# The output projection of each mixer layer in two turns by tokens, with the first turn's norm, residual and next inputs or stores beside the second

## The reference, cut to what matters

```
def merge_branches(...):
    m = (sigmoid(ga) * ((ya * silu(za)) @ w_branch[0]) + sigmoid(gb) * (...) + sigmoid(gc) * (...))
    return m @ w_o

def mixer_layer(x, ctx, ...):
    hx = rms_norm_2(x, g_pre) * (1.0 + scale_x) + shift_x
    hc = rms_norm_2(ctx, g_pre) * (1.0 + scale_c) + shift_c
    ... = in_proj(hx, w_in), in_proj(hc, w_in)
    ...
    out_x = merge_branches(...)
    x = x + gate_x * rms_norm_2(out_x, g_post)
    if update_ctx:
        ...
        ctx = ctx + gate_c * rms_norm_2(out_c, g_post)
    return x, ctx
```

## Time and profile before

| what | value |
|---|---|
| median of 3 runs | 2620.71 us (2618.78 to 2623.35) |
| the profiled execution | 2622.16 us, span 2620.4 us, mean granted TensorE clock 0.967 |
| PE busy | 2471.9 us, 94% of the span |
| DVE, ACT, POOL busy | 1179.1, 916.0, 531.7 us |
| chain that ended last | PE 85%, DVE 6%, ACT 4%, POOL 2%, issue 2%, DMA 1% |

### The profile page before, as it was taken

The page is one execution under the profiler, slowest core; times in us unless marked ns, Lnnn a source line. Parts: engine busy times, 40 slices in busy tenths (PEclk is TensorE's granted clock), DMA queues, the critical chain, the costliest instruction groups (busy, mean ns, idle before and its releaser), DMA issues.

```text
span 2620.4 us, 34188 instructions
## 1 busy us (share of the span) xinstructions
PE 2471.9 (94%) x14039; PEld 1979.8 (76%) x14039; DVE 1179.1 (45%) x1849; ACT 916.0 (35%) x1576; POOL 531.7 (20%) x381
## 2 busy tenths in 40 slices
PE   7887888899999999999999999999989999999998
PEld 5665666677788876678877888888866677878876
DVE  3745555353433445562267223323457633733432
ACT  3324543242222234552146211113335533632223
POOL 3003222040200212230014110022332210321023
PEclk8997899899999999999999999999989999999998
DMA  5231133145443321001300212123021023023232
GB/s 166 65 115 33 33 118 125 64 153 169 133 140 97 104 63 41 25 17 49 97 25 2 65 57 81 46 67 113 27 85 33 25 65 113 9 65 109 76 110 83
DMA packets 195740, 200.60 MB, mean 77 GB/s; under 512 B 15832, under 2 KB 189624, under 8 KB 195330
## 3 DMA queue, kind: packets, MB, share of 16 engines
q1 hardware_dynamic: 191106, 178.23, 21.7%
q10 hardware_dynamic: 4480, 20.19, 2.0%
HBM read 187.92 MB, written 10.49 MB: 76 GB/s over the span
## 4 chain that ended last, share of the span: by engine, by line
PE 85%; DVE 6%; ACT 4%; POOL 2%; issue 2%; DMA 1%; POOLq 0%; ACTq 0%; SPq 0%; DVEq 0%
PE PS L719 20%; PE PS L720 20%; PE PS L722 20%; PE PS L837 5%; PE PS L867 4%; PE PS L851 3%; DVE WL L1888 1%; PE PS L798 1%; PE PS L910 1%; ACT WH L1317 1%; PE PS L966 1%; PE PS L923 1%; PE PS L937 1%; POOL RB L2638 1%; PE PS L775 1%
## 5 line engine op out<-in xcount | busy, mean ns | idle before, releaser
L719 PE MATMUL PS<-HH,WH 128*128 128x512 f32 (+2 forms) x2096 | 776.0, 370 | 13.4 <-POOL HL L2791 6.6
L720 PE MATMUL PS<-HL,WH 128*128 128x512 f32 (+2 forms) x2096 | 744.9, 368 | 0.0
L722 PE MATMUL PS<-HH,WL 128*128 128x512 f32 (+2 forms) x2096 | 675.2, 366 | 0.0
L1888 DVE TENSOR_TENSOR WL<-WB,WH 128x2048 fp32r<-128x2048 f32 (+3 forms) x158 | 324.1, 2051 | 676.0 <-ACT WH L1317 666.5
L719 PEld LDWEIGHTS PS<-HH,WH 128*128 128x128 f32 (+1 forms) x2096 | 394.2, 188 | 124.3 <-issue 11.1
L720 PEld LDWEIGHTS PS<-HL,WH 128*128 128x128 f32 (+1 forms) x2096 | 394.2, 188 | 73.5 <-issue 2.9
L722 PEld LDWEIGHTS PS<-HH,WL 128*128 128x128 f32 (+1 forms) x2096 | 356.9, 188 | 45.1
L1317 ACT ACTIVATE WH<-WB 128x2048 fp32r<-128x2048 f32 (+3 forms) x158 | 265.1, 1678 | 343.4 <-PE PS L722 275.7
L2663 POOL TENSOR_SCALAR SA<-SA,ST 128x768 f32<-128x768 f32 (+4 forms) x80 | 142.2, 1778 | 533.2 <-DVE ST L1969 533.2
L2638 POOL TENSOR_TENSOR RB<-RB,SA 128x512 f32<-128x512 f32 (+2 forms) x65 | 88.2, 1357 | 399.2 <-ACT SA L1336 330.2
L1957 DVE TENSOR_REDUCE ST<-PS 128x1 f32<-128x768 f32 (+4 forms) x176 | 129.9, 738 | 71.4 <-PE PS L837 57.9
(11 more groups left out here) (366 smaller groups left out, 3641.1 us busy)
## 6 DMA issues: line engine op xcount, KB each, us to landing
WB<-in_w_in_dram SPq DMA_DIRECT2D x61, 1024.0 KB, 5.1
WB<-in_w_ff_dram SPq DMA_DIRECT2D x32, 1024.0 KB, 5.5
WB<-in_w_mod_dram SPq DMA_DIRECT2D x24, 1024.0 KB, 5.3
WB<-in_w_branch_dram SPq DMA_DIRECT2D x24, 512.0 KB, 3.5
WB<-in_w_o_dram SPq DMA_DIRECT2D x8, 1024.0 KB, 5.1
WB<-in_w_in_dram SPq DMA_DIRECT2D x14, 512.0 KB, 5.0
XTc<-xd ACTq DMA_DIRECT2D x2, 3072.0 KB, 10.0
WB<-in_cmp_w_dram SPq DMA_DIRECT2D x4, 1024.0 KB, 5.6
```

What stands on the lines that cost most here:

```text
L719: pe.matmul(D[0:m, d + o:d + o + w], h, xh[:, o:o + w], start=first, stop=False)
L720: pe.matmul(D[0:m, d + o:d + o + w], h, xl[:, o:o + w], start=False, stop=False)
L722: t = pe.matmul(D[0:m, d + o:d + o + w], lo, xh[:, o:o + w], start=False, stop=last)
L1888: dve.tensor_tensor(b.of(WL[s % NH]), b.of(WB[b.n % NW]), b.of(WH[s % NH]).bitcast(F32), ALU.subtract).then_inc(*done("wl", s))
```

## The change

The output projection of each layer is done in two turns. In layer 0 the first turn (`x`) does the 512 latent tokens and the second (`c`) the 256 context tokens; in layer 1 the turns are tokens 0 to 255 and 256 to 511. The first turn takes the output tiles 0 to 7, the second 4, 5, 6, 7, 0, 1, 2, 3: weight blocks 2 and 3 are used while they are still split, and blocks 0 and 1 are loaded and split once more, so each layer has 6 loads and splits of `w_o` in place of 4. Both turns use two of the four PSUM buffers. Beside the second turn run, tile by tile in each queue (`beside`), the first turn's sums, norm, residual and, in layer 0, the next inputs of `x` (`next_inputs`, `next_high`), in layer 1 its transposes, copies and stores. In layer 1 `linear_pair("ql1")` needs only the inputs of `x`; the context's sums follow it, the context's inputs are made beside the third tile of `ql1` and the first part of `kvl1`, which is now done by token sides (`linear_sides`). Buffers in SBUF are laid out anew for this.

```diff
-        cut(f"o{l}", I["w_o_2"][l])
+        for u in range(6):
+            i = u if u < 4 else u - 4
+            name = f"o{l}" if u < 4 else f"o{l}c"
...
+        TURNS = {0: {"x": (0, NX, 0), "c": (NX, NC, 1)}, 1: {"x": (0, 256, 0), "c": (256, 256, 0)}}
+        LATE = (4, 5, 6, 7, 0, 1, 2, 3)
+        def beside(late, early):
+            early = iter(early)
+            for _ in late:
+                next(early, None)
+            drain(early)
...
-                linear_pair(f"ql{l}", hx(NT), nt, queries, ready)
-                drain(linear(f"ql{l}", hx(NT), nt, queries, parts=[1]))
...
+                    ps.order = [0, 1]
+                    linear_pair("ql1", hx(NT), nt, queries, lambda k: [next_low("x", k)])
+                    out_sums("c")
+                    tile = linear("ql1", hx(NT), nt, queries, parts=[1], pace=4)
+                    next(tile)
+                    next(tile)
+                    spread_columns("o0c", NC)
+                    spread_columns("h1c", NC)
+                    drain(tile)
+                    linear_sides("kvl1", 2, NT, lambda j: [("kvr_a" if j % 2 else "kvr_d", 1, j)],
+                                 lambda s, k: [next_low("c", k)] if s else [])
...
+                def between(j):
+                    if l == 0:
+                        if j == 4:
+                            out_sums("x")
+                        elif j == 5:
+                            spread_columns("o0x", NX)
+                        elif j == 6:
+                            spread_columns("h1x", NX)
+                    elif j == 4:
+                        last_sums("x")
+                    elif j == 5:
+                        spread_columns("o1x", 256)
+                    elif j in (1, 3):
+                        turn_out("x", j // 2)
+                ps.order = [0, 1]
+                drain(linear(f"o{l}", half("x"), TURNS[l]["x"][1], lambda j: [("ot_a", l, "x", j)],
                              lambda k: [("ml_d" if k % 2 else "ml_p", l, k)]))
+                drain(linear(f"o{l}", half("c"), 256, freed, parts=[2, 3], after=between, to=f"o{l}c"))
+                drain(linear(f"o{l}c", half("c"), 256, freed, after=between))
+            last_sums("c")
+            spread_columns("o1c", 256)
             for h in range(2):
+                turn_out("c", h)
```

More of the change, by code:

```diff
@@ L1293, in tensor_program, with half @@
-            for h in range(2):
[L1294 to L1300, removed]
+                def half(side):
+                    o, n, _ = TURNS[l][side]
+                    return lambda k: (HH[:, k, o:o + n], HL[:, k, o:o + n])
@@ new lines, in late_tiles, with early_steps @@
+                def late_tiles():
+                    for i, j in enumerate(LATE):
+                        out_tile("c", i, j)
+                        if i == 1:
+                            begin(f"o{l}", 3)
+                        elif i % 2 and i < 7:
+                            begin(f"o{l}c", i // 2 - 1)
+                        yield
+                def early_steps():
+                    if l == 0:
+                        out_roots("x")
+                        yield
+                        yield from next_high("x")
+                    else:
+                        root("o1x", 256, 1024)
+                        for _ in range(3):
+                            yield
+                        for h in range(2):
+                            yield
+                            yield
+                            act.wait_ge(*at("tr", "out", h, 0))
+                            act.activation(ot[:, 0, h * 512:(h + 1) * 512], P("out", h, 0)[:, 0:512], ACT.Copy).then_inc(*done("out_a", h, 0))
@@ L1845, in scalar_program @@
                 for j in range(8):
-                    if j % 2 == 0:
+                    if j % 2 == 0 and j < 6:
                         begin(f"o{l}", j // 2)
[L1848 to L1862, removed]
+                    out_tile("x", j, j)
@@ L2451, in vector_program @@
                     if j == 2:
+                        if l == 1:
+                            next_sums("c")
                         begin(f"ql{l}", 1)
+                        if l == 1:
+                            inputs = next_inputs("c")
+                            for _ in range(4):
+                                next(inputs)
                     dve.wait_ge(*at("sq", f"qn{l}", j))
@@ new lines, in late_tiles, with last_part @@
+                def late_tiles():
+                    for i, j in enumerate(LATE):
+                        if l == 0:
+                            cross("c", i, j)
+                        if i == 1:
+                            begin(f"o{l}", 3)
+                        elif i % 2 and i < 7:
+                            begin(f"o{l}c", i // 2 - 1)
+                        yield
+                def last_part(side, f):
+                    o, n, _ = TURNS[1][side]
+                    X = OT[:, f, o:o + n]
+                    dve.tensor_tensor(X, X, P("norm", f"o1{side}")[:, 0:n], ALU.mult).then_inc(*done("on", 1, side, f))
+                    if f % 4 == 3:
+                        dve.wait_ge(*at("on", 1, side, f))
+                        dve.tensor_tensor(XTc[:, f, o:o + n], XTc[:, f, o:o + n], OT[:, f, o:o + n], ALU.add).then_inc(*done("xt_d", 1, side, f))
```

400 lines of the change are left out of this document (285 added, 115 removed).

## The result

The changed kernel took 2630.62 us (median of 6 runs, 2628.49 to 2633.57), the kernel before 2620.87 on the same chip (6 runs, 2618.78 to 2625.04): ratio 1.0038, 95% interval 1.0028 to 1.0048. The forecast was 2624.4 us and no change; the kernel is slower, by 9 us. That lies inside the range of 2615 to 2633 but outside the 2618 to 2626 of the forecast's own case.

What follows compares the result with a forecast made beforehand. PE, 94% busy, was taken as the bound, so only its waits or slow running around the two output projections could be won; 0.4 + 4.5 - 1.2 = +3.7 us on the median 2620.7 gave 2624.4 us, range 2615 to 2633.

Steps and rivals of the forecast that it cites:

- the forecast's own case: Whole kernel: waits between queues in the second turn cost as much as the old wait; 2618 to 2626 us, chance 0.50.
- a layout at full clock: Layer 0's queues laid out step by step without clock loss: `kvl1` and sums end at X+90.2 against X+89.8, +0.4 us.
- the clock: Layer 0: low granted clock costs 2.5 us in the pair and 2 in the second turn, +4.5, from 1.7 to 8.
- X: End of the first turn on PE in layer 0, forecast at 1863.3; the second turn's steps are counted from it.
- The circle: Layer 0's second turn: ACT and DVE wait for each other, 11.6 us per two tiles, 12.7 with POOL.
- the exclusion of POOL and DVE: Layer 0's second turn: POOL and DVE steps never run together; without this `kvl1` ends about 4.5 us sooner.
- slices and 256-wide matmuls: Layer 1: six slices before an old wait lose 2.1 us, 16 tiles of 2.83 for 8 of 5.6 lose 0.4; +2.5.
- PE's extra work: Layer 1, inside and behind the second turn: sums 0.9, spread 0.5, transposes 2.0, small waits 0.3; +3.7 us.
- the end: Layer 1 behind the last tile: sums and spread 1.8, `OT` part 0.3, POOL residuals 3.8, transposes and copies 1.5; -7.4 us.
- So halving costs nothing: Layer 1: 256-wide matmuls go at 0.12 us against 0.23 for 512, so splitting each in two is free.
- The last copy starts about 1 us sooner: Sign for the kernel's end, in the changed profile: the last copy begins about 1 us earlier.
- The third rival: Clock sinks twice in layer 0: +8 clock, 2.0 ACT and DVE hand-overs, +9.2 in all, 2630 us; chance 0.36.

Runs made afterwards that it cites:

- e3: The changed kernel with the 48 matmuls summing the x tokens' squares over 64 columns of ones in place of one: 2625.98 us, ratio 1.0024 to before.
- e2: The changed kernel with ACT making each next input one tile later in its queue in layer 0's second turn: 2621.97 us, ratio 1.0008 to before.
- e9: The kernel of e8 with the 24 one-column matmuls of the c tokens over 64 columns too: 2609.70 us, ratio 0.9953 to before.
- e10: The kernel of e7 with the x and c sums over 64 columns: 2613.66 us, ratio 0.9968 to before.
- e4: The changed kernel with POOL's steps beside layer 0's second turn over 2 columns, leaving out most of these sums: 2627.15 us, ratio 1.0023 to before.
- e7: The changed kernel with the edits of e2 and e4 together: 2617.71 us, ratio 0.9990 to before.
- e5: The changed kernel with PSUM buffers behind layer 1's key-value tiles taken in order 2, 1, 3, 2, not 2, 0, 3, 1: 2625.27 us, ratio 1.0020 to before.
- e1: The changed kernel with layer 1's projection back in one turn of 512 tokens, layer 0 still in two: 2627.94 us, ratio 1.0029 to before.
- e6: The changed kernel with the edits of e2 and e3 together: 2620.45 us, ratio 1.0000 to before.
- e8: The changed kernel with the edits of e1, e2, e3 and e5 together: 2614.84 us, ratio 0.9974 to before.
- e11: The changed kernel itself, unedited, measured again: 2630.32 us, ratio 1.0029 to before.

## Why the prediction was off

*Layer 0: right in mechanism and nearly in size.* Forecast +0.4 and, against a layout at full clock, +4.5 for the clock; from the end of the old wait to the 32-row product measured 138.2 in place of 133.0, +5.2. Counted from X = 1862.08:

| step | forecast | measured |
|---|---|---|
| end of the 48 one-column matmuls | 8.0 | 9.9 |
| end of tile 5 | 10.8 | 14.3 |
| first input of `x` done | 18.6 | 22.7 |
| a round of two tiles | 12.7 | 12.0, 12.2 |
| pair begins | 51 | 53.2 |
| pair ends | 62.2 | 66.4 |
| `kvl1` begins | 71.3 | 75.6 |
| `kvl1` and its sums end | 90.2 | 94.3 |

The forecast column leaves the clock out; with its 4.5 it ends at 94.7. (The prediction's "wait of 23 us in front of the pair" is a misreading that enters no sum: from 1883.84 to 1908.94 it is 25.1, most of it sums and spreads, with a wait of 5.88.) The clock cost 3.2 at the sums and tile 5 (11.4 against 8.2 in e3; forecast 2.0) and 2.0 in the pair (13.2 us against 11.2; forecast 2.5). The circle was shown by e2, the clock by e3 and e9 (and e10 agrees), the exclusion of POOL and DVE by e4 and e7: with POOL's steps thin DVE needs 8.4 us less. The rows agree: a DVE step that meets a POOL step ends behind it by its own duration less 0.14 to 0.20. A `cross` of 0.42 alone ended 0.28 behind POOL's low part (1915.33 + 0.89 against 1914.67 + 1.27, changed kernel), the split of 2.29 in e2 2.15 behind. That was the point where the Trainium skill (SBUF — State Buffer, on the shared port pair) was weighed; the exclusive lock that it states agrees with these rows. As a term of the sum, up to the end of `kvl1` and its sums, it was worth 2.1 to 2.5 (e4) and not 4.5.

*Layer 0, not in the sum.* Behind `kvl1` L0 loses another 1.1 us, and 1.05 of the 5.2 are a wait for `KVL`. The change takes the last PSUM buffers in another order, and both query sums and both `kvl1` tiles come at its very end; ACT reads the second one behind the root. I had followed PE's queue to the end of `kvl1` and stopped there. e5 shows the buffers to be the cause: with them in another order the wait for `KVL` is gone and the stretch behind it is 2.5 us shorter, more than the 1.1 that the change had lost there.

*Layer 1: the step that failed.* Forecast: +2.5 (slices and 256-wide matmuls), +3.7 (PE's extra work), -7.4 (the end), together -1.2. Measured +9.3 and -7.1. The win was sized right: POOL's six residuals took 4.52 us in place of 8.31. The cost was too small by 3.1, and the rows say where: 256-wide matmuls went 0.1204 us apart (168 from 2570.79 to 2591.02) against half of 0.233, which is 1.4 us for the 366 behind the wait and not 0.4; PE waits 1.10 for a weight split, which two tiles of 2.9 us no longer cover as two of 5.6 did; and 0.78 for a copy to `ot` in front of the last sums. "So halving costs nothing" was read from four matmuls and rounded. These three are read from the rows and were not tested apart; e1 tests their sum.

*The signs.* "The last copy starts about 1 us sooner" was wrong with the layer 1 term: it starts 60.6 us behind the last inputs (2564.07 to 2624.70) in place of 57.6. Also wrong: DVE's `cross` steps of the second turn took 0.43 to 0.90 beside POOL, and none took over 1 us, which fits a POOL term that was laid out too large. The other signs came as written: second turn 53 us, PE waits of 17.2 us for ACT's `OT`, last tiles 4.7, 7.3 and 4.9 us apart, clock low, first matmuls of the pair 0.43 apart, no wait for the context's inputs that holds up `kvl1`.

*The number.* 2624.4 was the sum +3.7. With the measured terms it is +6.3 and +2.2, 8.5. The third rival gave 2630 and so fits the time, but not by its mechanism: it wanted 8 us of clock and 2 of hand-overs with layer 1 at -1.2; the clock cost 5.2, the rounds were shorter than laid out, and the rest is layer 1 and the buffers. That the time fell inside the range is due to this rival's room, not to its reason, and so partly luck.

## What to carry to other kernels

When work is put beside other work in queues that run in order, write down for each pair of queues who reads first: here one step too early in ACT's queue cost 8 us. Taking it back brought the kernel level with the one before (1.0008), and with the other mends it came to 0.9953, where it was 1.003 to 1.004 without any. Two of those mends have nothing to do with the two turns, though, and were not tried on the kernel before: its 72 one-column matmuls took 12.2 us (1883.84 to 1896.07) where 72 at the pace of 16 in 1.79 would take 8.1, an estimate, and its PSUM buffers might be reordered too. How much of the 0.9953 is owed to the rearrangement is not shown. Follow every queue past the last edited line until the two kernels run alike, buffers included. And when a tile is halved, count what was hidden under its old length (a weight split, a copy), not only the matmuls.

## What the runs showed of the hardware

- Behind the first of 48 one-column matmuls in a row, 7 us with PE busy throughout, the granted clock fell to 0.5 (windows 0.55 and 0.60 of the changed kernel); the same 48 over 64 columns left it at 1.00. They cost the same: 16 took 1.79 us in both (1866.77 to 1868.56 in e3, 1865.76 to 1867.55 in the change, where the clock was still full).
- Behind the 24 one-column matmuls that follow the pair of tiles it fell in four profiles (e2, e6, e7, e8), all with e2's edit, and in none of the six without it (the change, e1, e3, e4, e5, e11); over 64 columns, in e9 and e10, it didn't fall there. Why those differ I can't say.
- DVE and POOL steps stood behind each other in both directions: a DVE split of 2.29 took 3.38 behind a POOL step, and a POOL add of 0.73 took 2.77 behind the split. A DVE step with one input in PSUM ran beside a POOL add at the full pace of both (e2, DVE and then POOL):

```profile
1904.18 0.74 DVE L2795 SCALAR_TENSOR_TENSOR SD<-XTc,GM,PS 128x512 f32<-128x512 f32 x1
1904.21 0.72 POOL L2873 TENSOR_TENSOR AC<-AC,SA 128x256 f32<-128x256 f32 x1
```

- The same stretch of the program repeats within 0.11 us in 13 profiles (579.01 to 579.12 us), while the median of the kernel before moved by 2 us between sessions. L0 itself moved by 0.7 us between profiles of the same layer 0. An effect of a few us is better read in such a stretch than in a ratio.
